# The tensors of the recurrent heads moved up by 96 bytes in each partition

## The reference, cut to what matters

```python
def hybrid_layer(x, ...):
    h = rmsnorm(x, g_mix)
    z = h @ w_in                       # 1024 x 7168
    rnn_x, rnn_y, conv_b, conv_c, conv_x, gate_rnn, gate_conv = split(z)
    rnn_x = causal_depthwise_conv(rnn_x, conv4_w) + conv4_b
    y_rnn = gelu(rnn_y) * rg_lru(rnn_x, w_rg_r, b_rg_r, w_rg_i, b_rg_i, lru_lambda)
    y_conv = conv_b * causal_depthwise_conv(conv_c * conv_x, conv3_w)
    merged = sigmoid(gate_rnn) * y_rnn + sigmoid(gate_conv) * y_conv
    x = x + merged @ w_out
    ...                                # feed-forward and a last gate
```

## The kernel before, in words

| tensors | past a multiple of 128 |
|---|---|
| stage, w_hi, w_lo, x, xs, xT_hi, xT_lo, aT_hi, aT_lo, cT_hi, cT_lo | 0 |
| the arena, xs_hi, xs_lo, ple_hi, ple_lo, xpad | 96 |
| cpad | 0 |
| y_sq and every recurrent tensor behind it: rx_hi, rx_lo, hT_hi, hT_lo, row_wide and the rest | 32 |
| first, second, third, place_of | 32 |

## Time and profile before

### The profile page before, as it was taken

One profiled execution on the slowest core, in us unless ns is written; L12 is line 12 of the kernel. 1 busy time (PEld: TensorE's weight loads), 2 busy tenths in 40 slices (PEclk: granted clock), 3 DMA queues, 4 the chain that ended last, 5 costly groups with the idle time before them and its releaser, 6 DMA issues.

```text
span 934.9 us, 13599 instructions
## 1 busy us (share of the span) xinstructions
PE 925.4 (99%) x5025; PEld 801.7 (86%) x5025; DVE 742.9 (79%) x1111; ACT 625.4 (67%) x953; POOL 20.5 (2%) x41
## 2 busy tenths in 40 slices
PE   9999999999999999999999999999999999999997
PEld 7888888888888888888888899999998888888886
DVE  6667687678999999999999889898897655555576
ACT  6685686676878778788777765747575544434456
POOL 2500000000000000000000000000000000000000
PEclk9999999999999999999999999999999999999999
DMA  9755427523799999999999364737457566555531
GB/s 341 243 183 187 148 91 253 174 70 136 250 371 372 354 363 374 356 366 375 353 365 325 99 198 157 251 114 243 154 186 244 184 201 198 180 180 180 187 129 45
DMA packets 102766, 214.50 MB, mean 229 GB/s; under 512 B 5672, under 2 KB 60480, under 8 KB 97088
## 3 DMA queue, kind: packets, MB, share of 16 engines
q1 hardware_dynamic: 101072, 211.70, 65.3%
q0 software_dynamic: 1344, 2.01, 0.8%
q10 hardware_dynamic: 304, 0.20, 0.1%
HBM read 212.84 MB, written 1.05 MB: 229 GB/s over the span
## 4 chain that ended last, share of the span: by engine, by line
PE 93%; DMA 2%; DVE 2%; ACT 1%; SPq 0%; issue 0%; DVEq 0%; ACTq 0%
PE bank L2367 20%; PE bank L2365 20%; PE bank L2366 20%; PE bank L3196 6%; PE bank L3198 6%; PE bank L3197 6%; PE bank L2382 4%; DMA stage<-in_cross_w_kv_dram 2%; PE bank L2378 2%; PE bank L2372 2%; PE bank L2373 1%; PE bank L2718 1%; PE bank L3223 0%; PE bank L3224 0%; PE bank L3222 0%; DVE w_lo L467 0%
## 5 line engine op out<-in xcount | busy, mean ns | idle before, releaser
L2365 PE MATMUL bank<-w_hi,xT_hi 128*128 128x512 f32 (+2 forms) x626 | 246.9, 394 | 0.0
L2367 PE MATMUL bank<-w_hi,xT_lo 128*128 128x512 f32 (+2 forms) x626 | 242.3, 387 | 0.0
L2366 PE MATMUL bank<-w_lo,xT_hi 128*128 128x512 f32 (+2 forms) x626 | 242.1, 387 | 0.0
L2367 PEld LDWEIGHTS bank<-w_hi,xT_lo 128*128 128x128 f32 x626 | 117.6, 188 | 24.0
L2365 PEld LDWEIGHTS bank<-w_hi,xT_hi 128*128 128x128 f32 x626 | 118.1, 189 | 21.9 <-DVE w_lo L467 0.2
L2366 PEld LDWEIGHTS bank<-w_lo,xT_hi 128*128 128x128 f32 x626 | 117.8, 188 | 22.0
L465 DVE TENSOR_TENSOR w_lo<-stage,w_hi 128x1024 fp32r<-128x1024 f32 (+3 forms) x94 | 107.4, 1142 | 30.2 <-ACT w_hi L451 28.8
L3196 PE MATMUL bank<-hT_hi,w_hi 128*128 128x256 f32 x440 | 123.7, 281 | 0.0
L3198 PE MATMUL bank<-hT_hi,w_lo 128*128 128x256 f32 x440 | 123.6, 281 | 0.0
L3197 PE MATMUL bank<-hT_lo,w_hi 128*128 128x256 f32 x440 | 123.5, 281 | 0.0
L451 ACT ACTIVATE w_hi<-stage 128x1024 fp32r<-128x1024 f32 (+3 forms) x96 | 95.5, 995 | 31.0 <-PE bank L2367 13.3
(11 more groups left out here) (488 smaller groups left out, 1520.8 us busy)
## 6 DMA issues: line engine op xcount, KB each, us to landing
stage<-in_w_in_dram SPq DMA_DIRECT2D x36, 1024.0 KB, 5.2
stage<-in_w_gate_up_dram SPq DMA_DIRECT2D x44, 512.0 KB, 4.7
stage<-in_expert_w_gate_dram SPq DMA_DIRECT2D x33, 512.0 KB, 5.5
stage<-in_expert_w_up_dram SPq DMA_DIRECT2D x33, 512.0 KB, 6.4
second<-in_expert_w_down_dram SPq DMA_DIRECT2D x16, 1024.0 KB, 6.8
stage<-in_expert_w_down_dram SPq DMA_DIRECT2D x15, 1024.0 KB, 7.1
stage<-in_w_down_dram SPq DMA_DIRECT2D x11, 1024.0 KB, 4.8
stage<-in_w_out_dram SPq DMA_DIRECT2D x8, 1024.0 KB, 6.0
```

The costliest lines, as they stand in the source:

```text
L2365: mm(o, k_hi, v_hi, start=start, stop=False)
L2366: mm(o, k_hi, v_lo, start=False, stop=False)
L2367: return mm(o, k_lo, v_hi, start=False, stop=stop)
```

## The change

```diff
--- before.py
+++ after.py
@@ -234,6 +234,7 @@
     def rb(name, shape, dt=F32):
         return recurrent_memory.enter_context(nc.sbuf_tensor(name, shape, dt))
 
+    rb("to_128_bytes", [P, 24])
     xpad = rb("xpad", [P, 2, 259])
     cpad = rb("cpad", [P, 2, 258])
     y_sq, y_in, y_tanh, c_in, q_inv, decay_a, u_in, states, gr_tanh, gc_tanh, merged = (
```

## The result

The changed kernel takes 938.54 us (median of 8 runs, 938.39 to 938.84) against 935.33 us for the kernel before (8 runs, 934.81 to 936.57). The ratio is 1.0029, with a 95% interval of 1.002 to 1.0037: slower by 0.2 to 0.4%. Its profiled execution took 938.84 us, of which 936.9 is the span; before it was 936.84 and 934.9.

What follows compares the result with a forecast made beforehand. The prediction took TensorE's matmul start rate to bound the heads. VectorE and ScalarE counted 0, TensorE's 1440 matmuls +1.9 us on the median 935.25, giving 937.2 us, with an 8-in-10 range of 930.5 to 938.6 us.

Steps and rivals of the forecast that it cites:

- The bound: In the four heads TensorE, busy all 42 us of each, sets the end by its matmul start-to-start rate.
- VectorE and ScalarE: In the heads, aligning their tensors was taken to cost or gain 0; at most 1.5 us without their spare time.
- The term: 1440 matmuls in the heads go from 118.66 to 120.0 ns start to start: +1.9 us, wholly on the path.
- The row with the same width: Last gate tile, 256 columns with both operands at multiples of 128: 120.0 ns a matmul, taken as the heads' new rate.
- The rows that spoke against it: Moving operands at 96 past a multiple of 128: 512 columns 233 ns, 6 more than aligned; 256 columns 118.0, 2 less.
- The base: Whole kernel: the term was added to the median of three timed runs, 935.25 + 1.9 = 937.2 us.
- Nothing moves: Rival: the heads' rate depends on operand roles, not addresses; time 935.3 us, chance 0.27.
- The cacheline rule: SBUF lines of 16 bytes: 96 bytes are six lines, so every operand crosses as many as before and nothing changes.
- Faster: Rival: aligned moving operands in the heads save 3 ns a matmul, 4.3 us, giving 930.9 us; chance 0.24.
- Slower by more: Rival: aligned reads in the heads clash with ring transfers or VectorE reads; 4.3 us more, 939.6 us, chance 0.07.
- The records: In head 1, matmul records would read 283 ns and the loads bracketing 276 matmuls lie 33.1 us apart.

Runs made afterwards that it cites:

- w at 32: w_hi and w_lo start 32 bytes past a multiple of 128, all else placed as in the kernel before; 956.15 us, ratio 1.0212.
- w at 64: Kernel before with w_hi and w_lo 64 bytes past a multiple of 128 and the change's pad, so hT and rx at a multiple; 950.32 us, ratio 1.0141.
- hT at 80: Kernel before with moving operands 64 bytes past a multiple of 128, but hT_hi and hT_lo at 80, in longer tensors; 938.01 us, ratio 1.0022.
- w at 32 with hT at 0: Kernel before with w_hi and w_lo 32 bytes past a multiple of 128, plus the change's pad of 24 float32; 955.99 us, ratio 1.0211.
- the heads at 64: Kernel before with a pad of 8 float32 ahead of xpad, so y_sq and those behind start 64 bytes past a multiple of 128; 935.45 us, ratio 0.9982.

## Why the prediction was right, and where not

**The bound.** Right. TensorE sets the end in the heads, and a longer start-to-start time shows in full: +1.80 us of heads in +2.0 us of span.

**VectorE and ScalarE.** Right: 692 and 693 ns, and the kernel with only their tensors aligned isn't slower.

**The term.** Right in size: +1.9 us forecast from 120.0 ns, +1.80 us measured, since the rate became 120.0 ns to the last digit. The row with the same width gave the right number, but in part by luck. What I called its cause was wrong: the gate tile stands at 120.0 ns because its two operands are at distance 0, and not because they are at a multiple of 128. The change happened to bring the heads to distance 0 as well. With w at 32 the same tile reads 118.7 or 117.4 ns, and with w at 64 113.3.

**The rows that spoke against it.** The worry that the stationary operand of the earlier trace rows was off a multiple of 128 as well was the better thought, and I left it there. place_of at 32 and xs at 96 are at distance 64, and 118.0 ns there is close to the 117.8 of that distance's two rates. ple at 96 over aT at 0 is at distance 96; with w moved, distances 32 and 64 read 234 and 233 ns for 512 columns too. So the sign does go by width: distance 0 is the best measured for 512 columns and, at 120.0 ns, level with the worst for 256.

**The base.** This is the step that was off. I set the sum on the median of three runs, 935.25 + 1.9 = 937.2, where the median became 938.54: inside the stated range of 930.5 to 938.6, but only just. By their times two of the three were executions at 117.3 ns and one at 118.6, and the sum was made for the profiled one at 118.6. Against its own execution the sum said 938.8, and the changed kernel's runs are 938.4 to 938.8. The change also ends that scatter: its 8 runs lie within 0.45 us. The loss is 2.0 us against an execution at the slower of the old rates and 3.5 us against the one at 117.3 (938.84 - 935.29). I had the 1.5 us between the runs before me and took it for noise.

**The rivals.** "Nothing moves" is refuted. The cacheline rule of the Trainium skill, "SBUF — State Buffer", "Door 1: The DMA port swizzle", would have had all of these kernels alike, since the steps are multiples of 16 bytes; the chip shows differences from 113.3 to 120.0 ns, and the measurement decides. "Faster" had the right magnitude for 512 columns and the wrong width. "Slower by more" didn't occur: 120.0 ns holds while the ring's transfers run at 188 GB/s.

**The records.** The duration of 283 ns and the 33.1 us for the bracket of 276 came as said: 120.0 x 276 = 33.1.

## What to carry to other kernels

For a product whose start-to-start time sets the end, read that time and not the duration, and compare it with another place of the same shape; note the start addresses of both operands there, not only of the one that the change moves. Keep 512-column operands at a distance of 0 modulo 128 from their stationary ones (226.7 ns against 233 or 234 here; the kernels that gave it up were 1.4 to 2.1% slower), and try 64 for 256-column ones (113.3 or 117.8 ns against 120.0), by measurement. When the runs of a kernel fall into two groups, find out which group the profiled one belongs to before a sum is set on the median.

## What the runs showed that I had not expected

- The start-to-start time of TensorE's matmuls depends on where the moving and the stationary operand start relative to each other. At distance 0 it is locked, at 120.0 ns for 256 columns and mostly 226.7 for 512: 106.7 ns for each 256 columns, and 13.3 ns beside them. At other distances it runs through a short repeating pattern: the kernel before has 116, 117, 120, 121, 120 ns in turn.
- One program at one distance has more than one such pattern: 118.6 and 117.3 ns at 32, 113.3 and 117.8 ns at 64. Most changes from one to the other stand behind a wait of TensorE, where two loads are 0.17 to 0.92 us apart instead of 0.12. Some come within the first 100 matmuls of the heads. Which pattern follows isn't settled by anything that was tried here.
- 120.0 ns isn't the mark of a lock. Two unlocked kernels, hT at 80 and w at 32 with hT at 0, have this mean too, and no kernel here settled at a rate above it. The spread of the single spacings shows the lock, and not their mean.
- Open: whether the distance counts modulo 128 or more. Two pairs of kernels with equal distances modulo 128 but not modulo 256 differ in rate (118.6 or 117.3 against 116.7 ns; 118.3 against a mean of 120.0), which fits a longer period; but several patterns at one distance would explain them as well. A third such pair speaks against the longer period: the heads at 64 and w at 64 with hT at 0 share the means 113.3 and 117.8. Distances of 0 and 128 modulo 256 weren't compared. Why the operands' places matter, no trace shows.
